# A hybrid decoder step on one Trainium2 core: VectorE takes state products and level factors earlier, and the score products of two key heads alternate

## The reference, cut to what matters

```python
# attention over the prompt, in blocks of 128 queries
s = jnp.einsum('bnqkgd,bnskd->bnkgqs', qb, kk) * (SWA_HEAD_DIM ** -0.5)
p = sink_softmax(s, mask[None, :, None, None], sinks...)
o = jnp.einsum('bnkgqs,bnskd->bnqkgd', p, vv)
...
# recurrence, in chunks; G is the running sum of log forget gates
o_inter = jnp.einsum('bchd,bhde->bche', qc * jnp.exp(G), S)
dec = jnp.where(causal, jnp.exp(jnp.where(causal, diff, 0.0)), 0.0)
A = jnp.einsum('bthd,btshd,bshd->bhts', qc, dec, kc)
o_intra = jnp.einsum('bhts,bshe->bthe', A, ic)
S_new = jnp.exp(G_last)[..., None] * S + jnp.einsum(
    'bshd,bshe->bhde', kc * jnp.exp(G_last[:, None] - G), ic)
```

## Time and profile before

| | us |
|---|---|
| median of 3 runs (1010.1 to 1010.88) | 1010.45 |
| the profiled execution | 1011.83 |
| its span, first to last instruction | 1010.0 |
| PE busy | 985.0 (98%) |
| PEld busy | 945.5 (94%) |
| DVE busy | 667.1 (66%) |
| ACT busy | 495.2 (49%) |
| POOL busy | 37.9 (4%) |

### The profile page before, as it was taken

How to read it: one execution, slowest core, us unless ns; L and a number is a source line. 1 busy time by engine, 2 the same in 40 slices (tenths; PEclk the granted TensorE clock), 3 DMA queues, 4 the chain that set the end, 5 groups by cost and what they waited for, 6 DMA issues and landing times.

```text
span 1010.0 us, 19271 instructions
## 1 busy us (share of the span) xinstructions
PE 985.0 (98%) x8110; PEld 945.5 (94%) x8110; DVE 667.1 (66%) x1035; ACT 495.2 (49%) x704; POOL 37.9 (4%) x60
## 2 busy tenths in 40 slices
PE   6999999999999999999999999999999999999998
PEld 5899998989999799999998999899899988999998
DVE  6677867757875655555656777867588666646463
ACT  6428562355574244535554296433737642535351
POOL 0050000000000000000000500000000000000000
PEclk9999999999999999999999999999999999999999
DMA  8453543333444384444463453433344443654542
GB/s 319 169 177 127 203 147 115 107 126 126 166 160 157 124 315 173 158 168 164 143 247 127 172 204 123 144 106 127 111 146 161 167 146 135 223 183 149 175 159 89
DMA packets 44021, 162.58 MB, mean 161 GB/s; under 512 B 5120, under 2 KB 6656, under 8 KB 43392
## 3 DMA queue, kind: packets, MB, share of 16 engines
q1 hardware_dynamic: 42512, 151.20, 42.6%
q0 software_dynamic: 1136, 9.63, 2.5%
q10 hardware_dynamic: 288, 0.52, 0.2%
HBM read 153.08 MB, written 10.29 MB: 162 GB/s over the span
## 4 chain that ended last, share of the span: by engine, by line
PE 92%; DVE 4%; issue 1%; ACT 1%; DMA 1%; SPq 0%; DVEq 0%; ACTq 0%
PE pz L396 81%; PE pm L396 10%; DVE w_lo L949 1%; DMA raw<-in_w 1%; ACT w_hi L717 1%; PE pm L522 1%; DVE arena L1219 0%; DVE arena L1168 0%; DVE arena L1169 0%; DVE h_lo L1251 0%; PE pm L580 0%; DVE arena L1239 0%; DVE arena L1205 0%; PE pm L570 0%; DVE arena L958 0%
## 5 line engine op out<-in xcount | busy, mean ns | idle before, releaser
L396 PE MATMUL pz<-a_hi,w_hi 128*128 128x288 f32 x1376 | 415.4, 302 | 10.9 <-DVE w_lo L1324 6.8
L396 PE MATMUL pz<-a_lo,w_hi 128*128 128x288 f32 x1376 | 406.9, 296 | 0.0
L396 PE MATMUL pz<-a_hi,w_lo 128*128 128x288 f32 x1376 | 405.7, 295 | 0.0
L717 ACT ACTIVATE w_hi<-raw 128x1024 fp32r<-128x1024 f32 x267 | 278.6, 1052 | 231.1 <-PE pz L396 226.3
L949 DVE TENSOR_TENSOR w_lo<-raw,w_hi 128x1024 fp32r<-128x1024 f32 x267 | 327.0, 1225 | 24.5 <-ACT w_hi L717 24.4
L396 PEld LDWEIGHTS pz<-a_hi,w_hi 128*128 128x128 f32 x1376 | 259.0, 188 | 15.6 <-DVE w_lo L1324 6.8
L396 PEld LDWEIGHTS pz<-a_lo,w_hi 128*128 128x128 f32 x1376 | 259.5, 189 | 1.1 <-issue 0.8
L396 PEld LDWEIGHTS pz<-a_hi,w_lo 128*128 128x128 f32 x1376 | 260.0, 189 | 0.0
L396 PE MATMUL pz<-h_hi,w_hi 128*128 128x288 f32 x768 | 229.8, 299 | 0.6 <-DVE h_lo L1251 0.6
L396 PE MATMUL pz<-h_lo,w_hi 128*128 128x288 f32 x768 | 226.6, 295 | 0.0
L396 PE MATMUL pz<-h_hi,w_lo 128*128 128x288 f32 x768 | 225.8, 294 | 0.0
(11 more groups left out here) (165 smaller groups left out, 550.1 us busy)
## 6 DMA issues: line engine op xcount, KB each, us to landing
raw<-in_w SPq DMA_DIRECT2D x267, 512.0 KB, 3.5
arena<-in_s SPq DMA_DIRECT2D x2, 2048.0 KB, 9.5
out_ss_out<-arena POOLq DMA_DIRECT2D x2, 2048.0 KB, 8.4
out_u_out<-arena POOLq DMA_DIRECT2D x2, 864.0 KB, 7.6
arena<-in_kcT SPq DMA_DIRECT2D x2, 512.0 KB, 7.8
arena<-in_vc SPq DMA_DIRECT2D x2, 512.0 KB, 6.0
out_kc_out<-in_kc_kept POOLq DMA_DIRECT2D x1, 992.0 KB, 6.7
out_vc_out<-in_vc_kept POOLq DMA_DIRECT2D x1, 992.0 KB, 8.7
```

The costliest lines, as they stand in the source:

```text
L396: return nc.tensor.matmul(out, a, b, start=start, stop=stop, **kw)
L717: act_fn(w_hi[:, r], raw[:, r], ACT.Copy).then_inc(s["w_hi"], 1)
```

## The change

DVE's reading of the state products and `keep_diagonal` move from turn 33, ahead of the level factors, to the end of turn 32, behind the differences of level 0. The level factors move into a function of their own, `level_factors`, which the loop calls in odd turns 33 to 45 ahead of `read_tile` and `split`; its instructions and waits are those of before. On PE, the score products of the two key heads alternate: in turn 11 the first query blocks of both heads (banks 0 and 1) and the first pair of each (banks 2 and 3), in turn 13 the second pair of each (banks 0 and 1), behind one wait for both of DVE's first reads. DVE reads the groups in the order 0, 1, 2, 4, 3, 5.

```diff
+SCORES = (0, 1, 2, 4, 3, 5)
...
                 if u in (11, 13):
-                    for g in ((0, 1, 2, 3) if u == 11 else (4, 5)):
-                        if g >= 4:
-                            pe.wait_ge(s["score_read"], l * 7 + (g - 3))
-                        if g < 2:
-                            for j in range(GRP):
-                                last = mm(PM[g][:, j * P:(j + 1) * P], qkv[kvr[g], j, 0:P], qkv[kvr[g], 4, 0:P])
-                        else:
-                            kv, j0 = (g - 2) // 2, 2 * (g % 2)
-                            for a in range(2):
-                                last = mm(PM[g % 4][:, a * NP:(a + 1) * NP], qkv[kvr[kv], j0 + a, P:NP],
-                                          qkv[kvr[kv], 4, 0:NP])
-                        last.then_inc(s["score"], 1)
+                    if u == 13:
+                        pe.wait_ge(s["score_read"], l * 7 + 2)
+                    if u == 11:
+                        for j in range(GRP):
+                            for kv in range(KV):
+                                last = mm(PM[kv][:, j * P:(j + 1) * P], qkv[kvr[kv], j, 0:P], qkv[kvr[kv], 4, 0:P])
+                                if j == GRP - 1:
+                                    last.then_inc(s["score"], 1)
+                    j0, b0 = (0, 2) if u == 11 else (2, 0)
+                    for a in range(2):
+                        for kv in range(KV):
+                            last = mm(PM[b0 + kv][:, a * NP:(a + 1) * NP], qkv[kvr[kv], j0 + a, P:NP],
+                                      qkv[kvr[kv], 4, 0:NP])
+                            if a == 1:
+                                last.then_inc(s["score"], 1)
...
-                for g in {12: (0, 1), 13: (2, 3), 14: (4, 5)}.get(u, ()):
-                    dve.wait_ge(s["score"], 7 * l + (g + 1))
+                for k in {12: (0, 1), 13: (2, 3), 14: (4, 5)}.get(u, ()):
+                    g = SCORES[k]
+                    dve.wait_ge(s["score"], 7 * l + (k + 1))
...
+            def level_factors(l, u):
+
+                i = (u - 33) // 2
...
+                dve.wait_ge(s["level_e"], 7 * l + (i + 1))
...
+                tt(x0, level_views(KK, m)[0], d0, ALU.mult).then_inc(s["level_x"], 1)
+                tt(x1, level_views(ZQ, m)[1], d1, ALU.mult).then_inc(s["level_x"], 1)
...
-                if u == 33:
-                    dve.wait_ge(s["sfin"], l + 1)
...
                     tt(d1, g1, ref, ALU.subtract).then_inc(s["level_d"], 1)
-                if 33 <= u <= 45 and u % 2:
...
+                if u == 32:
+                    dve.wait_ge(s["sfin"], l + 1)
+                    dve.wait_ge(s["ends"], l + 1)
+                    dve.wait_ge(s["i_tr"], l + 1)
...
+                    tt(ZI[:, 0:512], ZI[:, 0:512], PM[1], ALU.add).then_inc(s["sfin_read"], 1)
+                    dve.wait_ge(s["at_zero"], 2 * l + 2)
+                    keep_diagonal(l)
...
+                    if 33 <= u <= 45 and u % 2:
+                        level_factors(l, u)
                     if u < U_BR and (l > 0 or u > 0):
                         read_tile(l, u)
```

More of the change, by code:

```diff
@@ L1017, in attention @@
                     pv = prob[:, g].rearrange("p (a n) -> p a n", a=hs)
-                    stt(pv, PM[g % 4].rearrange("p (a n) -> p a n", a=hs), HD ** -0.5, mask, ALU.mult,
+                    stt(pv, PM[k % 4].rearrange("p (a n) -> p a n", a=hs), HD ** -0.5, mask, ALU.mult,
                         ALU.add).then_inc(s["score_read"], 1)
-                    dve.wait_ge(s["score_read"], 7 * l + (g + 1))
+                    dve.wait_ge(s["score_read"], 7 * l + (k + 1))
                     o = g * 4 if g < 2 else 8 + 2 * (g - 2)
@@ L1073, in pooling @@
                             ALU.subtract).then_inc(s["oc_lo"], 1)
+            def level_factors(l, u):
+                i = (u - 33) // 2
+                m = LEVELS[i]
+                D = (D0, D1)[i % 2]
+                X = (X0, X1)[i % 2]
+                dve.wait_ge(s["level_e"], 7 * l + (i + 1))
+                if i == 0:
+                    dve.wait_ge(s["ends"], l + 1)
+                if i == 1:
+                    dve.wait_ge(s["cross"], l + 1)
+                if i >= 2:
+                    dve.wait_ge(s["level_mm"], 11 * l + (i + 1))
+                d0, d1 = level_views(D, m)
+                x0, x1 = level_views(X, m)
+                tt(x0, level_views(KK, m)[0], d0, ALU.mult).then_inc(s["level_x"], 1)
+                tt(x1, level_views(ZQ, m)[1], d1, ALU.mult).then_inc(s["level_x"], 1)
             def hgrn(l, u):
@@ L1153, in hgrn @@
                     tt(d1, g1, ref, ALU.subtract).then_inc(s["level_d"], 1)
-                if 33 <= u <= 45 and u % 2:
[L1155 to L1169, removed]
+                if u == 32:
+                    dve.wait_ge(s["sfin"], l + 1)
+                    dve.wait_ge(s["ends"], l + 1)
+                    dve.wait_ge(s["i_tr"], l + 1)
+                    for h in range(H):
+                        last = ts_(ZI[:, h * P:(h + 1) * P], PM[0][:, h * P:(h + 1) * P], ep[:, h:h + 1], None,
+                                   ALU.mult)
+                    chain(last)
+                    tt(ZI[:, 0:512], ZI[:, 0:512], PM[1], ALU.add).then_inc(s["sfin_read"], 1)
+                    dve.wait_ge(s["at_zero"], 2 * l + 2)
+                    keep_diagonal(l)
                 if u == 35:
```

## The result

Four runs of the changed kernel took 998.35 us in the median (998.13 to 999.44), and four of the kernel before 1010.28 (1009.96 to 1010.88): ratio 0.9883, 95% interval 0.9869 to 0.9897. That is 11.9 us less. The prediction had 1001.1 with a range from 999.2: right in sign, 2.8 us short in size, and the range's lower end was missed by 0.9. Repeated beside other kernels, the changed kernel took 998.91 (998.61 to 999.17, four runs) against 1011.17.

A forecast was written before the change was run, and what follows sets the result against it. PE, 92% of the chain, was taken to bound the kernel. Parts 1 and 3 give 7.1 us, part 4 2.2: 9.3 off the profiled 1011.83 is 1002.5, less 1.38 for the median 1001.1; range 999.2 to 1004.0.

The forecast's parts named there:

- part 1: Turns 32 to 34: earlier state block ends PE's waits of 1.48 and 0.74 us in turn 34, 2.4 us per layer.
- Part 2: Turns 35 to 43: factors come first, reads and splits about 1.2 us later, where PE waits for nothing; zero gain.
- slower: In all seven odd turns DVE's read and split wait behind ACT's exponential, making DVE the bound: 1015 us, chance 0.03.
- Part 3: Turns 44 to 46: factor waits of 0.51 and 0.66 us go, sample copy wait becomes 1.3; 1.15 us per layer.
- Part 4: Score products of turns 11 and 13: alternating heads overlap, 0.96 us each, leaving 1.1 us per layer after waits and ACT.
- upper bound: Score products of turn 11: the most that alternating the heads could save, 1.1 us, where 0.96 was taken.
- the new wait in turn 13: PE, arriving earlier in turn 13, must wait for DVE's second score read, losing about 0.6 us.
- The take-back by ACT: Turn 22: PE's sample transposes need ACT's copy, so unit 14's 1.3 us early start falls back to 1.1 per layer.
- strict program order: Score products: if matmuls start and end in program order, alternating saves 0.9 us more per layer; 999.3 us, chance 0.03.
- The sample copy is not late: Turn 46: DVE has less to do, so the 1.3 us wait goes too, 2.6 in all; 998.5 us, chance 0.04.

The follow-up runs named there:

- e4: Kernel before, with eight products of constants that nobody reads filling PE's two waits of turn 34: 1009.13 us, ratio 0.9988.
- e1: Kernel before with only the change's score product edits for turns 11 to 14: 1007.26 us, ratio 0.9967.
- e2: Kernel before with only the state block moved from turn 33 to the end of turn 32: 1004.1 us, ratio 0.9939.
- e3: Kernel before with only the level factors moved ahead of tile read and split: 1004.16 us, ratio 0.9939.
- e9: Kernel before with e4's filler products in turn 34 and five more in PE's waits of turn 46: 1008.54 us, ratio 0.9967.
- e6: Changed kernel with DVE's masked copies of turns 45 and 47 ahead of tile read and split: 995.32 us, ratio 0.9846.
- e5: Changed kernel where PE in turn 34 also waits for level 1's differences, which it doesn't need there: 1008.19 us, ratio 0.9957.
- e8: Changed kernel with e6's reordering and the splits of turns 12 and 15 behind the score reads: 993.84 us, ratio 0.9831.

## Why the prediction was wrong in size

**The step that failed** stands in part 1: "PE then finds everything ready at 154.6: the 1.48 and the 0.74 go, plus about 0.1 each", 2.4 us per layer. It priced an idle of PE at its own length and took the work behind it at full speed. In the kernel before, the products of turn 34 behind the waits and the start of unit 35 ran at the 1.2 GHz level for 3.4 us, which cost another 1.33 and 1.52 us in the profiled execution. The mean granted clock of 0.997 stood below the table ahead of the prediction and I read it as nothing: on 1010 us it is 3 us. It was left out of the sum, of the rivals and of the range. The step mis-sized nothing else: at full clock the term measured 2.49.

**Part 2** held: units 36 to 44 take the same time, and DVE's later splits made PE wait nowhere. So the rival "slower", DVE standing for ACT in all pairs, did not come.

**Part 3** held: 1.17 to 1.18 us against 1.15, and the sample copy became the last wait, 1.17 us where I had 1.3.

**Part 4** held in its sum, 1.19 to 1.21 us against 1.1, by steps that were off both ways. Turn 11 gave 1.07 (forecast 0.96, upper bound 1.1), and the new wait in turn 13 was 0.63 (forecast 0.6), but turn 13's products gave 0.79, not 0.96, so units 12 to 14 won 0.16 instead of 0.36. The take-back by ACT was 0.03 where I had allowed some 0.2. ACT's chain doesn't show room for that: it began 1.2 us early itself (its first exponential starts at 78.64 us for 80.65; of these 2.01 us 0.81 are the start-up), where I had the maxima 1.05 early.

The Trainium skill ("TensorE: Matmul & The Clock Gate", Part 3) states strict program order for the starts and ends of matmuls. The change adds no evidence on it: by it turn 11 would now take 1.85 us, and the measured 2.03 is near that, but 8 narrow and 4 wide records in each half, my own account, make 1.84 too. What speaks against it lies in the kernel before: the 3.03 us, and a wide record of group 2 that starts at 58.37 us in the trace, ahead of the last narrow one of group 1 at 58.70, though it comes later in the program.

**The sum.** The profiled pair closes: 1011.83 - 9.7 - 2.85 - 0.81 (start-up) = 998.5, against 998.37 measured. Of the 2.75 us by which the medians came out lower than 1001.1, 0.4 is 9.7 in place of 9.3, and about 2.1 is the clock, by e4's runs at 1.000; the rest is within the spread of the runs. The clock's 2.85 may not be taken off the median: the 1.38 us by which the median lay below the profiled execution is the size of one fall. That the median executions before had one fall less is likely by their times, which are those of later runs at 0.998, and is not shown, as their clock is not on record.

**A number met by luck.** The rival "The sample copy is not late" had 998.5, nearest of all to the result, but its mechanism did not come: PE stood 1.17 us for that copy.

**Not settled:** why the same idle brings the clock down in one layer and not in the other (e1), and in some runs only. I know its price per fall from rows, not its rule. Where the clock fell in the runs of e2 and e3 at 0.998 was not profiled; that it was turn 46 in e2's, as in e4, is argued and not shown.

## What to carry to other kernels

An idle of PE may cost more than its length: look at the granted clock in windows of a microsecond or two behind each of PE's longer waits, compare the clocks of several runs with the profiled one's, and turn a mean of 0.997 into microseconds before calling it nothing. When a spread of some us in a kernel's times goes with the mean granted clock of the runs, test it with a few products that compute nothing in the waits (e9): what they win is the clock's share, the rest is the wait's. And on an engine that serves a busier one, put what that one waits for next ahead of what it needs two units later; then look for what has become last (the sample copy here, e6).

## What the runs showed that I had not expected

- Two idles of 1.48 and 0.74 us with 0.44 us of work between them were followed in the kernel before, in both layers, by about 3.4 us at 0.50; such a fall cost 1.3 to 1.5 us. In e5, behind 2.88 us of idle, one lasted some 7 us and cost 2.7.
- The fall moves: held up in turn 34, the clock fell in e4 behind the 0.64 and 1.05 us of turn 46. In e8, where no wait is left in either turn, it fell once at 114 us in the profiled run; the other three runs were at 1.000. PE had no idle ahead of that one: 30 records of small products ran for 5.37 us without a break, and the products of a unit followed at once. So idle isn't all that can go ahead of a fall. PE's timeline there and the windows, columns as above:

```profile
108.03 5.37 PE L397 MATMUL pm<-arena 128*64 128x512 f32 x30
```

```profile
110.00:114.00 4.00, 4.00 (x29) 2.87 (x25) 3.83 (x5) 2.55 (x6) 0.00 (x0) 1.00 0.60 202
114.00:118.00 4.00, 4.00 (x21) 4.00 (x20) 1.37 (x3) 0.01 (x1) 0.00 (x0) 0.57 0.03 11
```
